# A product moved from VectorE to ScalarE in the expert stage of a diffusion backbone

## What is computed

```
idx = jnp.take_along_axis(cand_i, top_pos, axis=-1)
g = jax.nn.softmax(top_s, axis=-1)
a = jax.nn.gelu(jnp.einsum('tkd,td->tk', jnp.take(u_tab, ib, axis=0), tb))
return jnp.einsum('tk,tkd->td', gb * a, jnp.take(v_tab, ib, axis=0))
```

## The kernel before, in words

| step of the prompt's mixing, layer 1 | slot | what it waits for |
|---|---|---|
| K(0), K(1): keys, copied out by ScalarE (L1446) | 241, 242 | |
| S(0), S(1): scores on TensorE (L1064) | 244, 246 | both the q and the K copies |
| T(0), T(1): transposes of the probabilities (L1071) | 248, 250 | VectorE's normalised probabilities (L1851) |
| mt(0), mt(1): transposes (L930), copied by ScalarE (L1367) | 384, 385 | |
| out(0): output projection on TensorE (L757) | 386 | the copies mt(0), mt(1) |

## Time and profile before

### The profile page before, as it was taken

The page is one execution under the profiler, slowest core; times in us unless marked ns, Lnnn a source line. Parts: engine busy times, 40 slices in busy tenths (PEclk is TensorE's granted clock), DMA queues, the critical chain, the costliest instruction groups (busy, mean ns, idle before and its releaser), DMA issues.

```text
span 5152.0 us, 37623 instructions
## 1 busy us (share of the span) xinstructions
PE 4042.2 (78%) x11663; PEld 1906.6 (37%) x11663; DVE 3140.8 (61%) x7049; ACT 521.8 (10%) x1158; POOL 2525.1 (49%) x2570
## 2 busy tenths in 40 slices
PE   8889889893887777777788988989277777777777
PEld 4674543341323333333343545334122222222223
DVE  1155877667555665654554678766766666665553
ACT  1130320100001001000000224001000000000000
POOL 0003345403665665665565234550177676676674
PEclk9889999996998999999999989999699999999999
DMA  8536679718999998999998466993299999999997
GB/s 264 168 120 223 211 265 329 270 49 281 399 398 349 371 363 346 371 395 370 355 398 297 163 208 221 334 318 101 96 381 408 352 374 389 374 375 378 368 409 287
DMA packets 578101, 1562.80 MB, mean 303 GB/s; under 512 B 51104, under 2 KB 246256, under 8 KB 576626
## 3 DMA queue, kind: packets, MB, share of 16 engines
q0 software_dynamic: 368640, 1342.34, 68.8%
q1 hardware_dynamic: 208690, 217.90, 12.9%
q10 hardware_dynamic: 576, 0.16, 0.0%
HBM read 1557.44 MB, written 2.79 MB: 303 GB/s over the span
## 4 chain that ended last, share of the span: by engine, by line
PE 32%; DMA 31%; DVE 14%; POOL 13%; issue 7%; DVEq 2%; ACT 1%; SPq 0%; PEldq 0%; PEld 0%; POOLq 0%; ACTq 0%
DMA rows<-in_peer_u_dram,idx 15%; DMA rows<-in_peer_v_dram,idx 15%; POOL rows L2056 13%; PE ps L1213 10%; PE ps L757 5%; DVE rows L1941 4%; PE ps L1103 4%; PE ps L740 3%; DVE work L1983 2%; PE ps L767 1%; PE ps L802 1%; PE ps L1106 1%; DMA ring<-in_w_in_dram 1%; DVE work L1894 1%; PE ps L1007 1%
## 5 line engine op out<-in xcount | busy, mean ns | idle before, releaser
L1213 PE MATMUL ps<-rows,work 128*128 128x512 f32 x4096 | 2014.7, 625 | 662.3 <-DMA rows<-in_peer_v_dram,idx 616.0
L1941 DVE CUSTOM_DVE_ANT_0 rows<-rows,ps 128x1024 f32<-128x1024 f32 x1024 | 1248.7, 1220 | 1140.3 <-DMA rows<-in_peer_u_dram,idx 1129.1
L2056 POOL DMA_INDIRECT rows<-in_peer_u_dram,idx x1280 | 1252.9, 979 | 1336.7 <-DVE idx L1934 805.6
L2056 POOL DMA_INDIRECT rows<-in_peer_v_dram,idx x1280 | 1271.5, 993 | 1263.5 <-PE ps L1213 536.2
L1213 PEld LDWEIGHTS ps<-rows,work 128*128 128x128 f32 x4096 | 738.7, 196 | 1859.5 <-issue 1396.7
L757 PE MATMUL ps<-h_s,ring 128*128 128x512 f32 x1024 | 451.9, 596 | 3.8 <-DMA ring<-in_w_in_dram 3.8
L1941 DVE CUSTOM_DVE_ANT_0 rows<-rows,work 128x1024 f32<-128x1024 f32 x256 | 312.6, 1224 | 152.7 <-DMA rows<-in_peer_u_dram,idx 145.8
L2020 DVE TENSOR_SCALAR work<-cst,acts,g_w 128x128 f32<-128x128 f32 x1024 | 369.8, 363 | 37.6 <-PE ps L1213 22.6
L1983 DVE SCALAR_TENSOR_TENSOR work<-rows,acts,work 128x1024 f32<-128x1024 f32 x254 | 325.7, 1282 | 4.8
L757 PE MATMUL ps<-work,ring 128*128 128x512 f32 (+1 forms) x768 | 276.8, 515 | 59.7 <-DMA ring<-in_w_branch_c_dram 34.2
L757 PEld LDWEIGHTS ps<-h_s,ring 128*128 128x128 f32 x1024 | 196.4, 192 | 255.1 <-issue 250.4
(11 more groups left out here) (286 smaller groups left out, 3086.4 us busy)
## 6 DMA issues: line engine op xcount, KB each, us to landing
ring<-in_w_in_dram SPq DMA_DIRECT2D x72, 1024.0 KB, 11.4
ring<-in_w_ada_dram SPq DMA_DIRECT2D x48, 1024.0 KB, 7.7
ring<-in_peer_wq_dram SPq DMA_DIRECT2D x32, 1024.0 KB, 5.9
rows<-in_peer_u_dram,idx POOLq DMA_INDIRECT x1280, 7.3
rows<-in_peer_v_dram,idx POOLq DMA_INDIRECT x1280, 7.1
ring<-in_w_out_dram SPq DMA_DIRECT2D x16, 1024.0 KB, 12.2
ring<-in_tables_dram SPq DMA_DIRECT2D x10, 1024.0 KB, 8.0
ring<-in_w_branch_c_dram SPq DMA_DIRECT2D x16, 512.0 KB, 10.6
```

The source lines that it names most:

```text
L1213: mm = pe.matmul(y_acc[:, cols], diag[:, e % TOPK, :], rows[:, ROWS + s, cols], start=e == 0, stop=e == EXPERTS - 1)
L1941: dve.tensor_tensor_reduce(rows[:, s, :], rows[:, s, :], tok, 1.0, 0.0, ALU.mult, ALU.add, dots[:, e:e + 1]).then_inc(rows_u_free, 1)
L2056: pool.indirect_dma_start(rows[:, slot0 + s, :], None, table, bass.IndirectOffsetOnAxis(ap=idx[:, t % 2, e:e + 1], axis=0)).then_inc(came[ ...
```

## The change

VectorE no longer builds the diagonals. Once per head it multiplies the 16 gelu values by the 16 gates in place and signals `weights_ready`; ScalarE then builds each diagonal with one product of the identity matrix and one per-partition scalar, in the slot in which VectorE did it, and waits itself for the free buffer. ScalarE's order in the sample's stage is rewritten as one loop over slots; the steps `soft`, `head_acts` and `tile_sum` keep their slots. The prompt's expert tile is as before.

```diff
+        weights_ready = sem("weights_ready")
...
             def sample_tiles(l):
+                first = l * STILES * EXPERTS
                 yield from soft(tile_of(l, True), slot_of(l, True, SOFT_PART + 1 - PARTS))
-                for j in range(STILES):
-                    t, n = tile_of(l, True, j), j * EXPERTS
-                    for h in range(PH):
-                        if h == (FIRST_PART + PART_STEP * SOFT_PART) // TOPK and j + 1 < STILES:
-                            yield from soft(t + 1, slot_of(l, True, n + FIRST_PART + PART_STEP * SOFT_PART + 1))
-                        if h == 1 and j:
-                            yield from tile_sum(l, j - 1)
-                        yield from head_acts(t, h, slot_of(l, True, n + (h + 1) * TOPK))
-                yield from tile_sum(l, STILES - 1)
+                soft_at = FIRST_PART + PART_STEP * SOFT_PART + 1
+                for n in range(TOPK, STILES * EXPERTS + M_LAG):
+                    j, e = n // EXPERTS, n % EXPERTS
+                    if j < STILES - 1 and e == soft_at:
+                        yield from soft(tile_of(l, True, j + 1), slot_of(l, True, n))
+                    if n % TOPK == 0 and n <= STILES * EXPERTS:
+                        done = n // TOPK - 1
+                        yield from head_acts(tile_of(l, True, done // PH), done % PH, slot_of(l, True, n))
+                    w = n - W_LAG
+                    if 0 <= w < STILES * EXPERTS:
+                        yield slot_of(l, True, n)
+                        act.wait_ge(weights_ready, (first + w) // TOPK + 1)
+                        if w >= TOPK:
+                            act.wait_ge(rows_v_free, tile_of(l, True) * EXPERTS + w - TOPK + 1)
+                        slot = w % EXPERTS
+                        act.mul(diag[:, slot % TOPK, :], ident, acts[:, slot:slot + 1]).then_inc(diag_ready, 1)
+                    if (n - M_LAG + 1) % EXPERTS == 0 and n > EXPERTS:
+                        yield from tile_sum(l, (n - M_LAG + 1) // EXPERTS - 1)
...
                     w = n - W_LAG
-                    if w >= 0:
-                        j, e = w // EXPERTS, w % EXPERTS
-                        t = tile_of(l, True, j)
-                        if e % TOPK == 0:
-                            head_weights(t, e // TOPK)
-                        row = first * EXPERTS + w
-                        if w >= TOPK:
-                            before = w - TOPK
-                            dve.wait_ge(rows_v_free, tile_of(l, True) * EXPERTS + before + 1)
-                        dve.tensor_scalar(diag[:, e % TOPK, :], ident, acts[:, e:e + 1], g_w[:, t % 2, e:e + 1],
-                                          ALU.mult, ALU.mult).then_inc(diag_ready, 1)
+                    if w >= 0 and w % TOPK == 0:
+                        j, h = w // EXPERTS, w % EXPERTS // TOPK
+                        t, hs = tile_of(l, True, j), slice(h * TOPK, (h + 1) * TOPK)
+                        head_weights(t, h)
+                        dve.tensor_tensor(acts[:, hs], acts[:, hs], g_w[:, t % 2, hs], ALU.mult)\
+                            .then_inc(weights_ready, 1)
```

## The result

The changed kernel takes **5156.77 us** (median of 20 runs, 5145.16 to 5165.03), the kernel before, beside it on the same chip, 5146.98 us (20 runs, 5137.19 to 5160.73). The ratio is 1.0018, 95% interval 1.0010 to 1.0026: 9.3 us slower, 5 to 13. That is no change within the bound of 0.2%, though the interval excludes nil. The profiled execution took 5165.03 us (span 5163.1).

The account below looks back on a forecast made before the run. The DMA engines were taken to bound the sample's expert stages, with VectorE's time mostly slack. Terms of -7 + 7.8 + 2.7 + 2 = +5.5 us on the median of 5152.74 us gave 5158.2 us, range 5142 to 5172.

Parts of the forecast that it names:

- The new waits: In ScalarE's in-order queue, each head's first diagonal waits for VectorE's multiplication, delaying mixing copies; 7.8 and 2.7 us at two places.
- S(0): Prompt mixing step near slot 244: both K copies come late behind slot 242's diagonal; 2.7 us lost, between 0 and 4.4.
- out(0): Prompt mixing step at slot 386: its copy mt(1) comes late behind that slot's diagonal; 7.8 us lost, between 0 and 10.
- The backlog: Where mixing held ScalarE, one or two diagonals run ahead of a copy at some four places; 2 us lost, 0 to 4.
- The gain: Diagonals leaving VectorE save 7 us: 4 in late gathers, 2.1 in tile sums, 1.0 in TensorE's mixing waits.
- late gathers: GpSimd's gathers of U rows held back by VectorE's dot products, 23.0 us in all; 4 us gained, between 0 and 23.
- four waits of TensorE: TensorE's waits for VectorE in the prompt's mixing, each shortened by one diagonal of 0.26 us; 1.0 us gained.
- tile sums: Eight places where TensorE stops until VectorE adds the output's first half; one diagonal of 0.26 us less each, 2.1 us gained.
- Signs: Expected in the trace: VectorE's busy time down some 360 us, ScalarE's up some 400, DMA at 409 GB/s, table loads unchanged.
- The rivals: Faster by freed GpSimd gathers, 5138 us (0.15); slower by more in-order waits, 5169 us (0.22); late diagonals, 5182 us (0.05).
- The slower rival: ScalarE's in-order wait at slots 16h+18 costs at more than two places; +16.6 us, 5169 us; chance 0.22.

Follow-up runs that it names:

- e7: Changed kernel with all of ScalarE's diagonals one slot later; 6.7 us below the kernel before.
- e8: Kernel before with 16 diagonals per layer, all on VectorE (wrong weights), plus ScalarE's bare wait at each head's first diagonal; +11.3 us against the kernel before.
- e6: Changed kernel with ScalarE's diagonals four slots later, each built in two halves of 64 columns; 6.7 us below the kernel before.
- e1: Changed kernel with ScalarE's diagonals four slots later; 8.2 us below the kernel before.
- e9: Kernel before, unchanged, timed and profiled again as a control; ratio 1.0004 to the kernel before.
- e2: Kernel before, diagonals still on VectorE, with ScalarE only waiting for each head's first diagonal; +11.8 us against the kernel before.
- e3: Kernel before with VectorE building only 16 diagonals per layer (wrong weights) and ScalarE as before; 11.3 us below the kernel before.
- e12: Repeat of the changed kernel with ScalarE's diagonals four slots later; 5.2 us below the kernel before.

## Why the prediction was right, and where not

**The class and the size** came out: +9.3 us beside a forecast of +5.5, within the own range. It lies only 1 us inside the bound of 10.3 us, though, and its interval reaches beyond. **The new waits** were the right term, at the right two places, and at no third that costs. The four profiles with both gaps have 96.1 to 96.9 us in A and 101.5 to 102.7 in B; those without the gap in question have 91.9 to 93.6 and 90.5 to 92.5. That prices S(0) at 3.3 us (mean 96.4 less 93.1) and out(0) at 10.6 (102.1 less 91.5), 14 us where I had 10.5.

- **out(0), taken as 7.8.** After the end of the tile, 2381.68, TensorE resumed at 2398.50, 16.8 us later; before it was 8.8 (2378.81 to 2387.64). That is 8.0 us, the term as predicted. What I had not priced is the clock. The granted clock was 0.67 in the stretch of the gap and 0.81 in the one behind it, and the pair of products after the gap took 3.75 us where 1.96 is usual, the lower level (1.2 GHz) instead of the upper (2.4). So out(0) began 20.4 us after the tile's end instead of 10.6 us, 9.7 later. In the five profiles with this gap it began 20.2 to 21.4 us after the tile's end, in the nine without 9.2 to 10.6, so the 10.8 between the means is the price and not scatter. The windows of the changed kernel (columns as in the earlier trace rows):

```profile
2384.00:2388.50 4.50, 4.50 (x16) 2.18 (x14) 0.96 (x2) 0.59 (x1) 1.78 (x2) 0.88 0.11 18
2388.50:2398.50 10.00, 0.24 (x3) 0.03 (x1) 2.55 (x5) 0.97 (x3) 1.97 (x3) 0.67 0.58 202
2398.50:2408.00 9.50, 9.50 (x42) 6.23 (x43) 0.00 (x0) 0.20 (x1) 2.05 (x3) 0.81 0.39 119
```

- **S(0), taken as 2.7.** The gap is 4.14 us (I had 4.4); T(0)'s wait fell only from 7.42 to 6.97 us, so it absorbs 0.45 and not 1.7. Here too the clock adds what I had not priced: S(0) itself took 2.05 us instead of 1.05, with a granted clock of 0.50 from 1938 to 1941. Of these 5.1 us T(0) absorbs 0.45 and stretch A keeps 3.3; where the rest is made up is not shown. That K(1) also holds S(0) was wrong (e7), without effect on the sum, since K(0) stands behind the same wait.
- **The backlog, taken as 2 us.** It is there (before the tile sum at 1666.17 two diagonals ran ahead of the copy, at 1664.45 and 1665.87), but e8 without it is no faster than the changed kernel and e6 with twice of it no slower than e1. It is nearer 0.
- **The gain, taken as 7.** In this pair of profiles the late gathers fell from 23.0 us to 20.1 (28.1 + 13.9 us, less 73 x 0.30), 2.9 where I took 4. Worked out in the same way for every profile, they are 18.3 to 20.2 us in the ten with the relief (19.3 in the mean) and 23.0 to 24.7 in the three without (23.8): 4.5, near the 4 that I took. In the mixing, where I took 1.0 for four waits of TensorE, the wait for the query fell from 9.03 to 8.74 us; four more, where I had not looked, fell by 0.25 us each in layer 1's last norm, from 6.53 to 6.28. The **tile sums, 2.1 us**, don't show in this pair: TensorE's waits for the first half were 39.9 us in six before (18.7 + 21.2) and are 39.8 now. Over all profiles they are 39.3 us in the mean with the relief (37.4 to 41.0) and 40.3 without (39.9 to 40.8), 1.0 less for six, where 1.6 was forecast for as many, and within the scatter. What I had not seen: the dot in front of the adds waits for its row of U, before as now, so the adds start mostly by when that row lands. VectorE before and now:

```profile
4100.68 1.22 DVE L1941 CUSTOM_DVE_ANT_0 rows<-rows,ps 128x1024 f32<-128x1024 f32 x1 [1.51 <-DMA rows<-in_peer_u_dram,idx]
```

```profile
4114.18 1.22 DVE L1952 CUSTOM_DVE_ANT_0 rows<-rows,ps 128x1024 f32<-128x1024 f32 x1 [1.31 <-DMA rows<-in_peer_u_dram,idx]
4115.32 0.08 DVE L1952 DVE_READ_ACCUMULATOR2_ANT dots<- 128x1 f32 x1
4115.32 1.12 DVE L1964 SCALAR_TENSOR_TENSOR x_s<-ps,g_s,x_s 128x128 f32<-128x128 f32 x4
```

At the next two tiles that wait was 1.06 and 1.07 us before and is 2.17 and 2.11 now.

So the traces show 14 us lost. The pair of profiles shows 4 gained (+10), all profiles together 6 to 7 (4.5 + 1.0 + 1.0 + 0.3), which gives +7 to +8; +9.3 and +9.8 were measured, with intervals from 4 to 15. That the forecast came within 4 us is in part luck: the backlog that isn't there (2 us) stands in for some of the clock's cost.

**Signs.** VectorE's busy time fell by 282 us, not 360, and ScalarE's rose by 317, not 400: I had multiplied the count by the mean of one (363 and 390 ns), but neighbours overlap, as the 0.26 us of the earlier trace rows had already said for VectorE. The wait for U, the DMA's rate in the full stretches (410 GB/s), table loads (104 in both) and the gathers' 0.94 us are as forecast. That the diagonals' wait for a free buffer is always met was wrong (133.2 us in layer 1's stage), and harmless.

**The rivals.** GpSimd gained nothing (978 against 979 ns; 103 gathers over 1.5 us against 101). A gather beside L1926, a two-input instruction on SBUF, took 2.85 us at 4563.90 in the changed kernel as well. The lock of the Trainium skill (SBUF — State Buffer, "SBUF: two separate sides") may be at work there, which no run here tests; the diagonals took no part in it. The slower rival needed more places; two places cost 14 us, of the 17.3 from which it decides. No diagonal was late: the least lead was 8.8 us.

**What stays open** is where the relief shows in the stages. The five runs that have it without the gap before out(0) or S(0) stand 5.2 to 11.3 us below the kernel before, 7.6 in the mean (6.0 by the medians), and four of the five intervals exclude nil. The waits of their traces show some 6 us of it (late gathers 4.3, tile sums 0.8, last norms 0.9, the query 0.3), near the 7 of the prediction, if each late gather counts in full, which is not shown. Yet stage 0 lasts 1585.8 us in their mean against 1586.1 in the two profiles of before, and layer 1's stage 1404.1 us in the mean of the ten profiles with the relief, 1405.9 in the three without it (before, e9, e2), with single ones from 1398.6 to 1410.4. One profile of each kernel can't place some 3 us in each stage against that scatter. It is open too whether the relief is worth less beside the gaps: e3 and e2 add up to +0.5 and e8 with both stands at +11.3, a difference of 2 to 20 us by the intervals, while the late gathers of e8 (19.2 us) are as low as those of e3.

## What to carry to other kernels

When a product moves to an idle engine, its duration is the smaller question: here doubling it cost nothing that could be measured, and a bare wait with no work cost 12 us. Ask what the wait in front of it makes late, by reading the queue behind it for anything that a third engine stands still for; and if the buffers allow, place the moved work some slots behind its input. With 16 buffers and ten slots of lead there was room for four slots, and the same change then comes out 5 to 8 us below the kernel before instead of 9 above it. It was barely room: in the three profiles with four slots (e1, e12, e6) the tightest diagonal was finished 0.8 to 1.3 us before its product. One slot (e7) did as well within the intervals, and left 9.0 us.

## What was not expected of the hardware

A gap on TensorE costs more than its length. After 8.9 to 10.0 us without work the next pair of products took 3.75 us instead of 1.96, in all five traces with this gap. After 4.14 us S(0) took 2.05 us instead of 1.05. ScalarE's short instructions overlap: eight diagonals of 390 ns each took 2.45 us, 0.31 each. A diagonal of half the columns took 333 ns against 386 for a whole one; the Trainium skill's formula (ScalarE: Activation LUTs, "What ACT_TABLE_LOAD costs") gives an estimate of 332 ns, and the trace agrees.
